# Opening of a transformer kernel: x's squares summed by TensorE through products of ones with whole tiles, GpSimd's adds left out, bias rows in six banks

## What is computed

```python
def rms_norm(x, g):
    xf = x.astype(jnp.float32)
    y = xf * lax.rsqrt(jnp.mean(xf * xf, axis=-1, keepdims=True) + EPS)
    return (y * g.astype(jnp.float32)).astype(x.dtype)

c_act = jax.nn.silu(c)
mods = jnp.split(c_act @ w_ada[l] + b_ada[l], N_MOD, axis=-1)
sh1, sc1, gt1, sh2, sc2, gt2, sh3, sc3, gt3 = mods
h = modulate(rms_norm(x, g_ffn1[l]), sh1, sc1)
x = x + 0.5 * gt1[:, None, :] * swiglu(h, w1_gu[l], w1_down[l])
...
def head_bias(dist):
    return rel_bias[:, rel_bucket(dist)].reshape(HKV, G, *dist.shape)
```

## Time and profile before

| | |
|---|---|
| median of 3 runs | 2116.59 us (2114.49 to 2116.65) |
| profiled execution, its own time | 2120.84 us |
| its span, from the first to the last instruction | 2119.0 us |
| mean granted TensorE clock | 0.991 |
| PE busy, share of the span | 98% |
| first feed-forward product starts | 43.01 us |

### The profile page before, as it was taken

How to read it: one execution, slowest core, us unless ns; L and a number is a source line. 1 busy time by engine, 2 the same in 40 slices (tenths; PEclk the granted TensorE clock), 3 DMA queues, 4 the chain that set the end, 5 groups by cost and what they waited for, 6 DMA issues and landing times.

```text
span 2119.0 us, 30323 instructions
## 1 busy us (share of the span) xinstructions
PE 2075.5 (98%) x12246; PEld 1786.8 (84%) x12246; DVE 1386.3 (65%) x1998; ACT 813.9 (38%) x1180; POOL 47.1 (2%) x60
## 2 busy tenths in 40 slices
PE   7999999999999999999999999999999999999998
PEld 6888888878887777879998988788689888989897
DVE  7766665554324674577786867777566459769595
ACT  4222212422332563353342444567443433424243
POOL 2000000000000000000000000000020000000000
PEclk9999999999999999999999999999999999999999
DMA  9555543222222112223232223411133122322222
GB/s 367 215 194 198 198 172 144 82 100 99 99 99 80 60 41 99 80 80 111 89 119 94 104 87 112 160 41 41 40 120 139 40 80 96 113 87 110 101 99 110
DMA packets 36748, 238.41 MB, mean 113 GB/s; under 512 B 4454, under 2 KB 6758, under 8 KB 8872
## 3 DMA queue, kind: packets, MB, share of 16 engines
q1 hardware_dynamic: 35132, 232.10, 30.0%
q10 hardware_dynamic: 1516, 4.94, 0.6%
HBM read 230.73 MB, written 6.29 MB: 112 GB/s over the span
## 4 chain that ended last, share of the span: by engine, by line
PE 90%; DVE 5%; ACT 2%; issue 1%; DMA 0%; POOL 0%; SPq 0%; DVEq 0%; ACTq 0%
PE ps L655 89%; PE ps L1157 1%; DVE ada_acc L2495 1%; ACT w_hi L1586 1%; DVE w_lo L2313 1%; DMA ada_slot<-in_ada 0%; DVE act_lo L2370 0%; DVE w_lo L2861 0%; ACT act_hi L1586 0%; DVE w_lo L2680 0%; ACT normed L1586 0%; DVE normed L2382 0%; ACT act_full L1586 0%; DVE normed L2824 0%; DVE act L2824 0%
## 5 line engine op out<-in xcount | busy, mean ns | idle before, releaser
L655 PE MATMUL ps<-act_hi,w_hi 128*128 128x512 f32 (+1 forms) x1672 | 615.5, 368 | 4.8 <-DVE w_lo L2680 3.0
L655 PE MATMUL ps<-act_hi,w_lo 128*128 128x512 f32 (+1 forms) x1672 | 606.9, 363 | 0.0
L655 PE MATMUL ps<-act_lo,w_hi 128*128 128x512 f32 (+1 forms) x1672 | 599.6, 363 | 1.2 <-ACT act_hi L1586 0.9
L1586 ACT ACTIVATE w_hi<-raw 128x2048 fp32r<-128x2048 f32 (+3 forms) x206 | 339.3, 1653 | 304.8 <-PE ps L655 295.6
L655 PEld LDWEIGHTS ps<-act_hi,w_hi 128*128 128x128 f32 x1672 | 316.8, 190 | 56.8 <-DVE w_lo L2680 3.4
L655 PEld LDWEIGHTS ps<-act_lo,w_hi 128*128 128x128 f32 x1672 | 316.6, 190 | 50.4 <-DVE act_lo L3463 2.0
L655 PEld LDWEIGHTS ps<-act_hi,w_lo 128*128 128x128 f32 x1672 | 316.7, 189 | 49.4
L2313 DVE TENSOR_TENSOR w_lo<-raw,w_hi 128x2048 fp32r<-128x2048 f32 x102 | 235.5, 2308 | 50.1 <-ACT w_hi L1586 48.4
L655 PE MATMUL ps<-hid_hi,w_hi 128*128 128x512 f32 (+1 forms) x680 | 260.7, 383 | 2.8 <-DVE hid_lo L2851 1.7
L655 PE MATMUL ps<-hid_lo,w_hi 128*128 128x512 f32 (+1 forms) x680 | 259.6, 382 | 0.0
L655 PE MATMUL ps<-hid_hi,w_lo 128*128 128x512 f32 (+1 forms) x680 | 259.5, 382 | 0.0
(11 more groups left out here) (425 smaller groups left out, 3188.6 us busy)
## 6 DMA issues: line engine op xcount, KB each, us to landing
raw<-in_weights SPq DMA_DIRECT2D x176, 1024.0 KB, 4.8
ada_raw<-in_ada SPq DMA_DIRECT2D x30, 1024.0 KB, 4.9
ada_slot<-in_ada SPq DMA_DIRECT2D x6, 1024.0 KB, 14.6
bias_rows<-biasrow SPq DMA_DIRECT2D x8, 320.0 KB, 17.0
x<-in_x SPq DMA_DIRECT2D x1, 2048.0 KB, 8.2
table<-bias_rows ACTq DMA_DIRECT2D x1, 2048.0 KB, 9.5
result<-x SPq DMA_DIRECT2D x7, 256.0 KB, 2.2
kept_x<-x ACTq DMA_DIRECT2D x1, 1536.0 KB, 5.1
```

Of the source, the lines that this page charges most:

```text
L655: return nc.tensor.matmul(out, lhsT, rhs, start=start, stop=stop)
L1586: return nc.scalar.activation(out, in_, func, **kw)
```

## The change

PE now sums the squares itself. `x_sum(t)` multiplies a 128x128 tile of ones by the whole square of tile `t` (512 columns) and accumulates all eight in bank 6, so that each partition of the bank holds the row of sums. ACT copies one partition of it to `x_row`, and `x_columns()` turns that row into four columns with four products on one row of the array. GpSimd adds nothing in the opening. The bias rows use six banks in place of eight: a head has its own pair of banks out of three pairs, waits only for the copy of the head three before it, and the eight heads stand one by one, six ahead of the sums and two between them. ACT copies a bias row between every two squares. On DVE the reciprocal moves ahead of block 5 of `w_ada`; it stood behind it. All `keep_warm` calls become `stream` calls, with others added.

```diff
--- before.py
+++ after.py
@@ -49,7 +49,6 @@
 CMP = (AT["cmpk"], AT["cmpk"] + 1, AT["cmpv"], AT["cmpv"] + 1)
 ADA_BLOCKS = 9 * DT // 2
 ADA_FIRST = 8
-WARM = 3
 START = 2
 XPRE_NORM = 6
 SCORE_BANKS = (0, 1, 4, 5)
@@ -315,6 +314,7 @@
             return consts[:, KAT[name]:KAT[name] + width]
 
         ident = const("ident")
+        x_row = act32[0:1, 0, :]
         s_raw = spare[:]
         t_high_of, t_low_of = {1: t_hi, 2: t_hi3}, {1: t_lo, 2: t_lo3}
         s_high_of, s_low_of = {1: s_hi, 2: s_hi3}, {1: s_lo, 2: s_lo3}
@@ -334,6 +334,7 @@
         ada_in = [sem("ada_in0"), sem("ada_in1")]
         ada_step, ada_sum = sem("ada_step"), sem("ada_sum")
         ada_zero = sem("ada_zero")
+        row_sum, row_copied = sem("row_sum"), sem("row_copied")
         quarter_ready, ada_turned, ada_folded = sem("quarter_ready"), sem("ada_turned"), sem("ada_folded")
         filled, v_step = sem("filled"), sem("v_step")
         c_ready, mods_ready = sem("c_ready"), sem("mods_ready")
@@ -803,10 +804,10 @@
                 for _ in range(n):
                     mm(ps[:, 6, 0:P], ones[:], zeros[:, 0:P])
 
-            def stream(n):
+            def stream(n, bank=6):
 
                 for _ in range(n):
-                    mm(ps[:, 6, 0:256], ones[:].bitcast(F32R), zeros[:].bitcast(F32R))
+                    mm(ps[:, bank, 0:256], ones[:].bitcast(F32R), zeros[:].bitcast(F32R))
 
             def add_columns(src, blocks=NT, stop=False):
                 for i in range(blocks):
@@ -950,6 +951,32 @@
                             last.then_inc(early_used, 1)
                         if tile == DT - 1:
                             last.then_inc(block_done, 1)
+
+            def x_sum(t):
+
+                pe.wait_ge(sq_ready, t + 1)
+                last = mm(ps[:, 6, :], ones[:], square[t % 2] if t else sumsq[:], t == 0, t == DT - 1)
+                if 1 <= t <= 5:
+                    last.then_inc(sumsq_step, 1)
+                elif t == DT - 1:
+                    last.then_inc(row_sum, 1)
+
+            def x_columns():
+
+                pe.wait_ge(row_copied, 1)
+                for i in range(NT):
+                    last = mm(ps[:, 4, i:i + 1], x_row[:, i * P:i * P + P], ones[0:1, 0:1])
+                last.then_inc(ms_ready, 1)
+
+            def bias_row_sum(h):
+
+                if h >= 3:
+                    pe.wait_ge(brow_copied, h - 2)
+                k = 2 * (h % 3)
+                rows = slice(64 * (h % 2), 64 * (h % 2) + 33)
+                for first, end in ((0, S), (S, NDIST)):
+                    last = mm(ps[:, k + first // S, 0:end - first], relb[rows, h, :], selector[rows, first:end])
+                last.then_inc(brow_sum, 1)
 
             def ada_columns(g):
 
@@ -1266,31 +1293,30 @@
 
             pe.wait_ge(sel_in, 32)
             pe.wait_ge(relb_ready, 1)
-            for pair in range(4):
-                if pair >= 2:
-                    pe.wait_ge(brow_copied, 2 * pair - 2)
-                k = 4 * (pair % 2)
-                for first, end in ((0, S), (S, NDIST)):
-                    for u in range(2):
-                        rows = slice(64 * u, 64 * u + 33)
-                        last = mm(ps[:, k + 2 * u + first // S, 0:end - first],
-                                  relb[rows, 2 * pair + u, :], selector[rows, first:end])
-                last.then_inc(brow_sum, 1)
+            for h in range(6):
+                bias_row_sum(h)
+            for t in range(3):
+                x_sum(t)
+            bias_row_sum(6)
+            x_sum(3)
+            bias_row_sum(7)
+            for t in range(4, DT):
+                x_sum(t)
             pe.wait_ge(brow_copied, 8)
-            begin_stats()
-            pe.wait_ge(sq_ready, DT)
-            add_columns(square[0])
-            add_columns(square[1], stop=True).then_inc(ms_ready, 1)
+            stream(8, 7)
+            x_columns()
+            stream(8, 7)
             ada_columns(0)
+            stream(6)
             pe.wait_ge(ident_in, 16)
             pe.wait_ge(rinv_ready, 1)
             for i in range(NT):
                 last = mm(ps[:, 5, i * P:i * P + P], rinv[:, i:i + 1].to_broadcast([P, P]), ident)
             last.then_inc(rstd_ready, 1)
             norms[0] += 1
-            keep_warm(4 * WARM)
+            stream(36)
             ada_columns(1)
-            keep_warm(5 * WARM)
+            stream(20)
             ffn(0, AT["ffn1"], 0)
 
 
@@ -1955,25 +1981,23 @@
             act.wait_ge(cols_in, 16)
             fn(c_act[:], col("c", 0, DT), ACT.Silu).then_inc(c_ready, 1)
 
-            def bias_rows(pair):
-                act.wait_ge(brow_sum, pair + 1)
-                for u in range(2):
-                    k = 4 * (pair % 2) + 2 * u
-                    fn(biasrow[2 * pair + u][:], ps[:, k:k + 2, :].rearrange("p a n -> p (a n)")[:, 0:NDIST],
-                       scale=-1.0).then_inc(brow_copied, 1)
-
+            def bias_row(h):
+                act.wait_ge(brow_sum, h + 1)
+                k = 2 * (h % 3)
+                fn(biasrow[h][:], ps[:, k:k + 2, :].rearrange("p a n -> p (a n)")[:, 0:NDIST],
+                   scale=-1.0).then_inc(brow_copied, 1)
+
+            for h in range(3):
+                bias_row(h)
             act.wait_ge(x_in, 16)
-            for t in range(3):
+            squares(0, x[:, 0, :])
+            for t in range(1, 6):
                 squares(t, x[:, t, :])
-            bias_rows(0)
-            squares(3, x[:, 3, :])
-            bias_rows(1)
-            squares(4, x[:, 4, :])
-            bias_rows(2)
-            squares(5, x[:, 5, :])
-            bias_rows(3)
+                bias_row(t + 2)
             squares(6, x[:, 6, :])
             squares(7, x[:, 7, :])
+            act.wait_ge(row_sum, 1)
+            fn(x_row, ps[0:1, 6, :]).then_inc(row_copied, 1)
             take_root()
             act.wait_ge(raw_in[0], 16)
             for u in range(2):
@@ -2233,11 +2257,6 @@
 
         @block.gpsimd
         def _(pool):
-            for t in range(1, DT - 2):
-                pool.wait_ge(sq_ready, t + 1)
-                if t > 1:
-                    pool.wait_ge(sumsq_step, t - 1)
-                nc.gpsimd.tensor_tensor(sumsq[:], sumsq[:], square[t % 2][:], ALU.add).then_inc(sumsq_step, 1)
             for t in range(4):
                 pool.wait_ge(split_hi if t == 3 else second_quarter, 2 if t == 3 else t + 1)
                 pair = slice(2 * t, 2 * t + 2)
@@ -2942,13 +2961,13 @@
                 v.memset(nmx[k][:], 0.0).then_inc(block_used, 1)
 
             dve.wait_ge(c_ready, 1)
-            for b in range(6):
+            for b in range(5):
                 ada_first_block(b)
             norms[0] += 1
             dve.wait_ge(root_ready, 1)
             v.reciprocal(rinv[:, 0:NT], root[:, 0:NT]).then_inc(rinv_ready, 1)
-            ada_first_block(6)
-            ada_first_block(7)
+            for b in range(5, 8):
+                ada_first_block(b)
             first_low(0)
             modulation(0, 2)
             gain(0, 1, "g_ffn1").then_inc(mods_ready, 1)
```

## The result

The changed kernel takes 2121.72 us, the median of 20 runs (2117.07 to 2123.46); the kernel before took 2117.22 in the same runs (2114.29 to 2120.07). The ratio is 1.0018, 95% interval 1.0011 to 1.0024: the change costs about 4 us (4.5 between the medians), which is just inside the 0.2% that counts as no change. The forecast was 2115.9 with a range up to 2120.2, so the time lies above it. The profiled execution took 2121.97, its span is 2120.2, its mean granted clock 0.991.

A forecast was written before the change was run, and what follows sets the result against it. PE was taken to bound the weight loop, so the shift of `mods` counts in full: 39.83 - 38.8 = 1.0 us off the median 2116.59 gives 2115.6, rounded up to 2115.9 us; range 2112.8 to 2120.2.

The forecast's parts named there:

- GpSimd's price: DVE's modulation in the opening: GpSimd's adds cost it 3.5 us, less what DVE would then wait for its blocks.
- Pace of PE, not the column: PE's opening: a sum costs 1.71 us until the clock rises, then 0.86, although the granted clock column reads 1.00.
- the 4.4 us: PE's sums: assumed time of work until the clock rises, at 18.2; the upper bound was 6.0.
- The root at 28.7: ACT's root behind sums, row copy and `x_columns`: due at 28.7 us, against 27.0 in the kernel before.
- Where the stall goes: Reciprocal to `mods`: DVE waits 3.1 us, its modulation and PE's list both end at about 36.8, GpSimd's gain taken back.
- 38.8: Forecast start of `mods` in us, from 36.9 + 1.88, against 39.83 in the profile before.
- The second rival: PE's clock stays low through the sums: rise near 30, root 33.3, `mods` 43.4, 2120.2 us; chance 19%.
- the 0.3 us: Rounding up from 2115.6 to 2115.9, because `keep_warm` may end up to 1.2 us sooner in the median of before.
- 48 products: PE's work in the profile before, between the reciprocal's release at 31.41 and the release of `mods` at 39.83.
- After `mods`: Behind the opening: `stream(20)`, 2.5 us, replaces `keep_warm(15)`, 3.59; SP is free at 35, and nothing new waits.

The follow-up runs named there:

- e11: Changed kernel with five 128x512 adds put back on GpSimd, into a tile that nothing reads; median 2119.68 us, ratio 1.0012 to the kernel before.
- e13: Changed kernel with stream(26) added behind the two products at the start, run again for a second profile; profiled execution 2113.18 us.
- e15: The kernel before, unchanged, run again for a second profile; profiled execution 2114.95 us.
- e1: Changed kernel, unchanged, run again for a second profile and as control; median 2120.47 us, ratio 1.0017 to the kernel before.
- e2: Changed kernel with stream(26) added behind the two products at the start; median 2116.76 us, ratio 0.9995 to the kernel before.
- e16: Changed kernel with heads 6 and 7 last, stream(26) at the start, ada_columns(0) with added streams ahead of the spread, stream(24) for stream(36); median 2118.81 us, ratio 1.0006.

## Why the prediction was wrong, point by point

- **GpSimd's price**: right. 3.5 us less DVE's waits were forecast; block 4 was through at 25.2 (forecast 25.5) in place of 27.18 + 1.29 = 28.5, with 1.285 for each operation.
- **Pace of PE, not the column**: right. The first sum took 1.87 us from start to start, heads ran side by side and ended at 14.1 (13.8). The time of the rise was luck: the 4.4 us were chosen below an upper bound, with no row behind them. They met the 18.1 of the first profile; the other two had 19.4, at the end of the range given.
- **The root at 28.7**: mis-sized by 0.9. The 28.7 is the root's end, which came at 29.31 + 0.27 = 29.58, in the other two profiles at 30.25 and 30.20, where the clock rose later. A head alone between sums took 1.27 from start to start in place of 1.07, and the sum between the two heads 1.06 in place of 0.86. DVE's end followed: 37.70 in place of 36.8, 0.9 us. PE's list behind `x_columns` followed too, from 29.20 on in place of 28.2.
- **"Where the stall goes. PE meanwhile: ... spread 1.0 ..., `stream(36)` 4.5; with the seams overlapped these end at about 36.8 too"**: this is the step that failed. It gave all of PE's list behind the root the high clock because the clock had risen once. It fell again for 3.4 us in each of the three profiles, and the list ended at 39.54 (40.20, 40.15). The step gave it 36.8 - 28.2 = 8.6 us; it took 10.34. e11 shows what the step assumed: with the clock up the same list takes 8.75, so the length was right and the pace was not. The start 1.0 late and a list 1.74 too long, less 0.1 of rounding, are the 2.6 us between 38.8 and 41.42. Why the clock falls in most executions and not in e11 or e13 stays open.
- **The second rival**, a clock that stays low, named the right resource and the wrong place: I looked for one change of the clock, a late rise, and priced no fall. The sum of that rival, 2120.2, is nearer than my own, but its course (a rise near 30, a root at 33.3) came in no profile.
- **The kernel before**: the 0.3 us allowed for a sooner rise was small. e15 has `mods` 1.0 sooner than the profile that the sum starts from. A slip beside it: the "48 products" behind 31.41 are 48 records, two to a product.
- **After `mods`**: right for the program (2078.8 against 2079.2; SP was free at 31.38, ahead of its weight load at 43.74).

The opening accounts for 1.6 us between the two profiles first taken, and for 2.5 between the means of three and two (41.84, 39.33). The medians differ by 4.5, or 3.9 in the runs of e1. In those runs the mean granted clock is 0.9932 for before and 0.9921 for the changed kernel. As an estimate, that is 0.0011 x 2120 = 2.4 us of the 3.9, and the fall in the opening (3.4 us at 0.50) makes 0.0008 of the 0.0011. The rest of the program has short low stretches of its own, at other places in each execution: between 45 and 2100 us the column shows about 31 and 17 us of them in the two profiles of before, and 27, 24 and 24 in those of the changed kernel. From `mods` to the end it took 2079.2 and 2074.4 before and 2078.8, 2077.6 and 2076.7 after. Whether the change makes them more frequent, or the three profiles merely missed the executions in which the opening fares worst, stays open. So of the 5.8 us between the forecast and the measured median, the profiles place 2.6 to 3.3 ahead of `mods`; the rest is not located.

## What to carry to other kernels

An engine's pace has to be priced for each stretch that it works in, not once from the point at which it rises, and one profile doesn't settle it: the same list of products kept its clock in e11 and e13 and lost it in seven other profiles. Before a wait is moved, ask who is second: here DVE's stall and PE's list of streams ended within 2 us of one another, so mending either alone brought nearly nothing in the medians and both together 4 to 5 us. And in a chain that crosses engines (head, copy, table load, square, sum), work that nobody needs yet belongs behind it, not in it.

## What the hardware showed that I had not expected

- The clock fell although PE had been busy for 12.68 of the 13.60 us before (changed kernel, 18.10 to 31.70). In e11 it stayed at 1.00 behind the same products with the same busy time. What tells the two apart is not shown.
- The raised clock fell during products on 33 rows in e2 (0.50 from 11.6 to 18.3), and not in e13 or e16, where the same 24 passes took 4.67 us.
- The granted clock reads 1.00 ahead of its first fall, even at half pace: 6 heads in 7.89 us in the changed kernel, in 4.67 in e13.
- One program's executions differ by up to 12 us (e16: 2111.51 to 2123.84) while their mean granted clock goes from 0.994 to 0.987, more than any edit here was worth.
